# The chunked recurrence of a two-block model on one core: other PSUM banks for the first updates of a head, state copies ahead of statistics, and a first step of an output group inside the last unit

## What is computed

```python
def step(carry, xs):                       # one chunk of one head, one direction
    C, n, m = carry
    ...
    s = einsum('bhtd,bhsd->bhts', qj, kj) * exp(log_D - m_t[..., None])
    num = einsum('bhts,bhse->bhte', s, vj) + inter_w[..., None] * einsum('bhtd,bhde->bhte', qj, C)
    den = sum(s, axis=-1) + inter_w * einsum('bhtd,bhd->bht', qj, n)
    h = num / maximum(abs(den), exp(-m_t))[..., None]
    C_new = decay[..., None, None] * C + einsum('bhs,bhsd,bhse->bhde', ws, kj, vj)
    n_new = decay[..., None] * n + einsum('bhs,bhsd->bhd', ws, kj)
...
h = h_fwd + h_bwd                          # then normalised per head, gated
h = h + einsum('bse,ed->bsd', y, w_out[l]) # output projection, residual
return rms_norm(h, norm_out_g)             # then the second block
```

## Time and profile before

| | us |
|---|---|
| median of 3 runs | 1175.57 (1175.13 to 1175.79) |
| the profiled execution | 1175.25 |
| its span | 1173.5 |
| PE busy | 1161.9 |
| DVE busy | 676.0 |
| POOL busy | 456.3 |
| ACT busy | 358.2 |
| the recurrence, first to last L1198 | 498.7 to 677.2 |

### The profile page before, as it was taken

How to read it: one execution, slowest core, us unless ns; L and a number is a source line. 1 busy time by engine, 2 the same in 40 slices (tenths; PEclk the granted TensorE clock), 3 DMA queues, 4 the chain that set the end, 5 groups by cost and what they waited for, 6 DMA issues and landing times.

```text
span 1173.5 us, 17251 instructions
## 1 busy us (share of the span) xinstructions
PE 1161.9 (99%) x6599; PEld 946.2 (81%) x6599; DVE 676.0 (58%) x1249; ACT 358.2 (31%) x720; POOL 456.3 (39%) x437
## 2 busy tenths in 40 slices
PE   9999999999999999999999999999999999999997
PEld 6888888888888878887878888888988887777786
DVE  5645557333277403067777874894698434555568
ACT  7312122100011112444674531242112034543322
POOL 3424222233342224344666665304224224454534
PEclk9999999999999999999999999999999999999999
DMA  8321121443212122301113242132121120142113
GB/s 240 118 72 45 36 81 36 129 152 116 100 36 72 64 72 81 100 23 28 47 35 128 68 171 72 73 122 76 53 70 36 56 80 1 38 157 87 37 38 142
DMA packets 75075, 93.56 MB, mean 80 GB/s; under 512 B 13938, under 2 KB 54090, under 8 KB 74483
## 3 DMA queue, kind: packets, MB, share of 16 engines
q1 hardware_dynamic: 67270, 88.73, 22.8%
q10 hardware_dynamic: 7724, 3.74, 1.2%
HBM read 75.11 MB, written 18.92 MB: 80 GB/s over the span
## 4 chain that ended last, share of the span: by engine, by line
PE 95%; DVE 1%; POOL 1%; issue 1%; ACT 0%; DVEq 0%; POOLq 0%; ACTq 0%
PE bank L912 24%; PE bank L914 23%; PE bank L913 23%; PE bank L1184 3%; PE bank L1205 3%; PE wide L1198 2%; PE wide L1394 2%; PE bank L1152 1%; PE bank L1141 1%; PE wide L914 1%; PE wide L913 1%; PE wide L912 1%; PE wide L1381 1%; PE bank L1369 1%; PE bank L1129 1%
## 5 line engine op out<-in xcount | busy, mean ns | idle before, releaser
L683 POOL CAST whi<-wraw 128x2048 fp32r<-128x2048 f32 x31 | 58.7, 1894 | 453.4 <-PE bank L914 402.6
L912 PE MATMUL bank<-u_hi,wlo 128*128 128x512 f32 x488 | 190.4, 390 | 0.0
L914 PE MATMUL bank<-u_hi,whi 128*128 128x512 f32 x488 | 189.9, 389 | 0.0
L913 PE MATMUL bank<-u_lo,whi 128*128 128x512 f32 x488 | 189.9, 389 | 0.0
L685 POOL TENSOR_TENSOR wlo<-wraw,whi 128x2048 fp32r<-128x2048 f32 x32 | 153.2, 4786 | 3.0 <-ACT whi L2467 0.5
L912 PE MATMUL bank<-x_hi,wlo 128*128 128x512 f32 x312 | 123.4, 396 | 0.0
L914 PE MATMUL bank<-x_hi,whi 128*128 128x512 f32 x312 | 121.6, 390 | 0.0
L913 PE MATMUL bank<-x_lo,whi 128*128 128x512 f32 x312 | 121.5, 389 | 0.0
L912 PEld LDWEIGHTS bank<-u_hi,wlo 128*128 128x128 f32 x488 | 91.6, 188 | 19.6 <-POOL wlo L685 0.8
L914 PEld LDWEIGHTS bank<-u_hi,whi 128*128 128x128 f32 x488 | 91.6, 188 | 19.1
L913 PEld LDWEIGHTS bank<-u_lo,whi 128*128 128x128 f32 x488 | 91.6, 188 | 19.0
(11 more groups left out here) (375 smaller groups left out, 2438.0 us busy)
## 6 DMA issues: line engine op xcount, KB each, us to landing
wraw<-in_w_in SPq DMA_DIRECT2D x26, 1024.0 KB, 5.4
wraw<-in_w_out SPq DMA_DIRECT2D x12, 1024.0 KB, 5.1
xr<-in_x SPq DMA_DIRECT2D x8, 512.0 KB, 7.0
hst<-in_x SPq DMA_DIRECT2D x4, 1024.0 KB, 5.2
hpool<-hst SPq DMA_DIRECT2D x4, 1024.0 KB, 4.1
smz<-mzs SPq DMA_DIRECT2D x16, 256.0 KB, 2.0
h<-hpool SPq DMA_DIRECT2D x4, 1024.0 KB, 6.9
resid<-h SPq DMA_DIRECT2D x8, 512.0 KB, 2.6
```

The lines of the kernel that those rows point to most:

```text
L683: g_.tensor_copy(whi[w % 2][:, :, :], wraw[:, :, :]).then_inc(s["w_hi"], 1)
L912: pe.matmul(ps, al, bh, start=(k == 0), stop=False)
L913: pe.matmul(ps, ah, bl, start=False, stop=False)
L914: return pe.matmul(ps, ah, bh, start=False, stop=(k == nk - 1))
```

## The change

Four edits.

The first update products of a head in the backward direction (p = 0, d = 1) take banks 0 and 2, where they took banks 2 and 3. All other updates keep banks 2 and 3.

On DVE, for heads 1 and 2, the copy of the first state update (`state(h, n)` in step 0, forward) moves out of the head's own `units` and to the end of the head before, behind its last two outputs and ahead of the means and statistics that stand there.

In the last unit, 63, PE first issues step k = 0 of the output group at place 2 of `ORDER` into bank 1 (`fill`). The other three steps follow behind the recurrence into the same bank, and the loop over the ring begins with place 3, with bank 0.

`ORDER` has tile 2 at place 2, where it had tile 4; tiles 4 and 5 move one place back. DVE adds the groups in that order.

```diff
-    ORDER = (0, 1, 4, 5, 2, 3, 6, 7)
+    ORDER = (0, 1, 2, 4, 5, 3, 6, 7)
@@ PE, units(h)
                     _, p, d, ck, r = unit(n)
+                    if n == 16 * NH - 1:
+                        ahead = fill("v_h2", len(AHEAD) + 1)
+                        group(W_OM, ORDER[len(AHEAD)], m_hi, m_lo, "v_h2", len(AHEAD) + 1, ks=range(1), ps=ahead)
                     if p:
...
                         for k in range(2):
-                            ps = take(2 + k, "v_C", 2 * m + k + 1)
+                            ps = take((0, 2)[k] if p == 0 and d else 2 + k, "v_C", 2 * m + k + 1)
@@ PE, behind the recurrence
+            group(W_OM, ORDER[len(AHEAD)], m_hi, m_lo, "v_h2", len(AHEAD) + 1, ks=range(1, 4),
+                  ps=bank[bank_of["v_h2", len(AHEAD) + 1]])
             pe.wait_ge(s["g_ymlo"], 8)
-            for i in range(len(AHEAD), NT):
+            for i in range(len(AHEAD) + 1, NT):
                 group(W_OM, ORDER[i], m_hi, m_lo, "v_h2", i + 1)
@@ DVE, units(h)
                     total(h, n)
-                    state(h, n)
+                    if p or h in (0, NH - 1):
+                        state(h, n)
                     total(h, n + 1)
...
                     output(h, n + 1)
+                    if p == NT - 1 and h + 1 < NH - 1:
+                        state(h + 1, n + 2)
```

## The result

| | before | after |
|---|---|---|
| median, us | 1175.53 (4 runs) | 1184.24 (1183.69 to 1184.83, 4 runs) |
| ratio | | 1.0073 [1.0061, 1.0086] |
| the profiled execution, us | 1175.25 | 1183.84 |
| its span, us | 1173.5 | 1181.9 |
| mean granted clock of TensorE | 0.999 | 0.997 |

The change costs 8.7 us; the forecast was 6.7 (1182.2), and the rival in which the clock falls had 1185.2. The page after answers to the earlier trace rows: busy time on PE grows by 0.8 us only, so most of the 8.4 us more of span are time in which PE stood still. (Matmuls at the lower clock count as busy. They hardly show in the sum, as the ten opening records took 4.89 us here and 6.14 in the earlier trace rows.)

The account below looks back on a forecast made before the run. PE's list of waits was taken to bound the kernel (busy 1161.9 of 1173.5 us). Heads 3.54 plus the end 3.13 made 6.67, so the median 1175.57 becomes 1182.2 us; range 1180.0 to 1185.6, forecast 63%.

Parts of the forecast that it names:

- The heads: Starts of heads 0 to 3: inter product waits for DVE's copy to free bank 0; 0.96, 0.77, 1.04, 0.77, sum 3.54 us.
- the signs it named: Idle ahead of L1187 in each head, some 4 us at L912; head 2 loses most; first-to-last intra product +3.6 us.
- The gap behind the recurrence: Group at place 4 waits for bank 1 until DVE adds place 2: PE idle 4.1 us, transposes +3.13 us.
- rival (a): PE's clock falls in the 4.1 us gap behind the recurrence; a 6.1 us low stretch loses some 3.05: 1185.2 us; 22%.
- The new order of tiles: Tile 2's rows land at 683.5 to 683.7, before DVE needs them at 685.6: no cost, 1.9 us cover left.
- What the edits could win: Existing PE waits: 0.68, 0.32, 0.51 at heads 1 to 3 and 1.05 at the recurrence's end; 2.56 us at most.
- case (c): Banks at the heads and behind the recurrence are free when PE asks; wins 1.51 + 1.05: 1173.0 us; 3%.

Follow-up runs that it names:

- the run of the edit alone: The kernel before with only the bank edit (backward first update of a head in banks 0 and 2): 1179.06 us, ratio 1.0029.
- the run of the step alone: The kernel before with only the output-group step in unit 63 and the new `ORDER`: 1181.55 us, ratio 1.0047.

## Why the prediction was right, and where it was off

*The heads.* Forecast 0.96, 0.77, 1.04, 0.77 (3.54); measured 0.96, 0.76, 1.02, 0.76 (3.50). In the run of the edit alone, where the copies stay in place, head 2 costs 0.77 and the sum is 3.26. The constant that carried it, 0.56 us from the start of DVE's copy to the start of the waiting matmul, came out the same at all four heads. Of the signs it named, head 2 does lose most, but the idle time ahead of L1187 reads 0.72 to 1.20, not 1.3 to 2.2, and the time from the first to the last intra product grows by 4.0, not 3.6; 0.4 of that is unit 59, below.

*The gap behind the recurrence.* Forecast: PE idle for 4.1 us. Measured: the last matmul's successor was due at 686.08 and started at 690.17, 4.1. What this adds to the time was put at 3.13. Measured it is 3.14: the lag grows from 3.88 to 8.53, and 1.51 of that is the clock.

*The clock.* The step that failed is the choice against rival (a). The forecast put the clock at nothing; it cost 1.5 us. The prediction gave the rival 22%, with "one drop is one case, and the two lengths are close" against it. It came: the clock fell at the end of an idle time of 4.1 us, and both kernels with the gap show it, while the kernel with PE at work in the same gap doesn't. The mean granted clock of each of their eight executions is 0.996 or 0.997, and 0.998 or 0.999 in the four of the third kernel, so it wasn't only the profiled one. The Trainium skill (TensorE: Matmul & The Clock Gate, "Why this matters for your kernels") advises against gaps over about 3 us, and the trace agrees, with 4.1. The price of the rival was mis-sized as well, twice over: 3.05 was half of 6.1 us, but the low stretch lasted 3.4 us in the changed kernel, and of the 6.8 us in the run of the step alone 1.4 fell into the idle time, where they cost nothing. Measured are 1.5 and 2.5. The opening was a poor measure of the length: the same ten records take 6.14 us in the earlier trace rows and 4.89 in the changed kernel:

```profile
1.03 4.89 PE L954 MATMUL bank<-ones 128*128 128x384 f32 x10 [1.03 <-POOL eps L690]
```

The measured 1184.24 lies in the range because the range had been drawn to hold this rival. That it is only 1 us from the rival's 1185.2 is partly luck: the 1.5 too much for the clock is in part made up by the 0.4 at unit 59, which no term had.

*What is left over.* 3.50 + 3.14 + 1.51 = 8.15 of the 8.53 us. The 0.38 that stay are the late total of unit 59, which costs PE 0.42, less a few hundredths that come back ahead of it. Its idle time reads 0.64 in the changed kernel as well:

```profile
666.77 0.43 DVE L1782 TENSOR_TENSOR wide<-wide,tmpi 128x257 f32<-128x257 f32 x1 [0.64 <-ACT tmpi L2402]
```

The prediction had no term for this.

*The new order of tiles* cost nothing, as forecast: DVE's two additions follow its list without an idle time for the rows of tile 2.

*What the edits could win*, put at 0.68, 0.32 and 0.51 at the heads and 1.05 at the end, was measured at 0.68, 0.24, 0.22 and 1.12 with free banks, 2.26 in all. The prediction's case (c), 2.56 us, was too high by what unit 50 takes back in head 3, and it left out the weight load that takes another part 100 us later. The risk would have shown in the profile before: ACT's split starts at 768.01, 1.2 us after a load lands that took 5.2, and the same kernel's loads before and behind it took 5.4 and 8.3.

## What to carry over

When a step is given another buffer, look up who uses that buffer next in the list: the wait for it moves to that instruction, and is as long as the reader of the buffer is late in its own list. Of an idle time on TensorE like the one of 4 us here, price two things, the wait and the slower matmuls behind it; only the part of the low stretch in which matmuls run costs anything. When a gain shows up at its place and not in the total, follow the lead of matched instructions down the trace; each step in it leads to the instruction that took it, though not always to a wait.

## What was not expected of the hardware

*An instruction of DVE that starts 0.35 us late, as it seems by its place in the list.* In six profiled kernels with the copies moved (the changed one and five of the runs) DVE sits idle for 0.63 or 0.64 us ahead of the total of unit 59; in the kernel before, in the run of the bank edit and in both of the step without the copies, for 0.28; and with 16 unrelated instructions ahead of it, for 0.28 again, in both kernels where that was tried. From the end of ACT's copy into `tmpi` to the start of the total it is 0.45 us in those six and 0.10 in the other six. Ahead of the total the traces list 829 records of DVE in the four, 831 in the six and 846 in the two. That the code of the instruction came late to the engine would fit it; no row shows this, and it stays a conjecture.

*A weight load of 1 MB that took 5.2 to 7.3 us from issue to landing* at the same place of the twelve profiled kernels. The four that come to it earliest, by 0.6 to 2.0 us, show the longest (6.9 to 7.3), the others 5.2 to 6.3; the fifth, 0.05 us behind the fourth, took 5.4. Each was seen once, so whether this is scatter or hangs on what else moves then is open.

*The clock doesn't fall at a fixed time after the last matmul.* In the kernel before it fell 3.5 us after the end of TensorE's last work, and this one case was all that the prediction had. In the gap it fell 3.7 us after the last matmul in the changed kernel and 2.5 in the run of the step alone, and at the ends of the twelve traces 2.8 to 4.7. So a gap of 4.1 us need not have made it fall each time, though it did in both kernels.

*The opening scatters by more than a microsecond.* From 20 us into the span to the first head the traces keep a constant distance to the kernel before, between 0.31 us ahead and 1.17 behind, with the same instructions up to there. Leads of a few tenths can only be read with this taken off.
